# Sample attention stream: one cast per chunk on VectorE, and ScalarE's key copies and accumulator moves ahead of the exponential

## What is computed

```python
def fox_attention(q, k, v, fq, fk, q_pos, k_pos):      # one block of it
    s = jnp.einsum('bqhd,bkhd->bhqk', qi, k) * scale
    s = s + fi.transpose(0, 2, 1)[..., :, None] - fk_t[..., None, :]   # cumulative log forget values
    s = jnp.where(mask, s, -jnp.inf)
    p = jax.nn.softmax(s, axis=-1)
    return jnp.einsum('bhqk,bkhd->bqhd', p.astype(v.dtype), v)
```

## Time and profile before

| what | value |
|---|---|
| time, median of 3 runs | 4010.86 us (4007.85 to 4014.97) |
| the profiled execution | 4007.52 us |
| its span, first to last instruction | 4005.8 us |
| busy: TensorE, VectorE, ScalarE, GpSimd | 3686.3, 2013.1, 1706.0, 1070.8 us |
| granted TensorE clock, mean | 0.970 |
| GpSimd's `low_values` | 256 subtractions, 609.6 us |
| VectorE's `high_values` | 256 casts, 380.2 us |

### The profile page before, as it was taken

How to read it: one execution, slowest core, us unless ns; L and a number is a source line. 1 busy time by engine, 2 the same in 40 slices (tenths; PEclk the granted TensorE clock), 3 DMA queues, 4 the chain that set the end, 5 groups by cost and what they waited for, 6 DMA issues and landing times. The chain is left out here.

```text
span 4005.8 us, 55888 instructions
## 1 busy us (share of the span) xinstructions
PE 3686.3 (92%) x19019; PEld 2961.9 (74%) x19019; DVE 2013.1 (50%) x3175; ACT 1706.0 (43%) x3409; POOL 1070.8 (27%) x764
## 2 busy tenths in 40 slices
PE   8999999999999999988999996878888888699999
PEld 7788888887788888866787884555566666488887
DVE  3234433322134433214443436889898888744432
ACT  4224434554225335434344444555566666412222
POOL 0011222220011223201000003555566666422200
PEclk9999999999999999997998997989999999899999
DMA  4233343333233343313100007878898888644422
GB/s 157 99 108 116 121 148 131 118 116 105 94 124 131 127 158 106 128 57 95 43 1 12 12 1 257 259 240 265 256 297 286 279 284 285 228 159 165 166 84 82
DMA packets 354282, 590.76 MB, mean 147 GB/s; under 512 B 44029, under 2 KB 90213, under 8 KB 354026
## 3 DMA queue, kind: packets, MB, share of 16 engines
q1 hardware_dynamic: 340722, 576.00, 43.6%
q10 hardware_dynamic: 12736, 9.32, 0.8%
q0 software_dynamic: 576, 2.10, 0.1%
HBM read 475.38 MB, written 111.96 MB: 147 GB/s over the span
## 5 line engine op out<-in xcount | busy, mean ns | idle before, releaser
L853 PE MATMUL prj_z_ps<-prj_w_hi,prj_h_hi 128*128 128x512 f32 x2312 | 923.4, 399 | 2.6 <-DVE prj_w_lo L677 2.6
L855 PE MATMUL prj_z_ps<-prj_w_hi,prj_h_lo 128*128 128x512 f32 x2312 | 902.0, 390 | 0.0
L854 PE MATMUL prj_z_ps<-prj_w_lo,prj_h_hi 128*128 128x512 f32 x2312 | 900.8, 390 | 0.0
L1688 POOL TENSOR_TENSOR sa_v_lo<-sa_v_raw,sa_v_hi 128x1024 fp32r<-128x1024 f32 x256 | 609.6, 2381 | 416.7 <-DVE sa_v_hi L1860 416.7
L855 PEld LDWEIGHTS prj_z_ps<-prj_w_hi,prj_h_lo 128*128 128x128 f32 x2312 | 434.1, 188 | 93.6
L853 PEld LDWEIGHTS prj_z_ps<-prj_w_hi,prj_h_hi 128*128 128x128 f32 x2312 | 434.9, 188 | 89.7 <-DVE prj_w_lo L677 5.5
L854 PEld LDWEIGHTS prj_z_ps<-prj_w_lo,prj_h_hi 128*128 128x128 f32 x2312 | 435.0, 188 | 84.7
L2031 PE MATMUL sa_t_ps<-sa_ident,sa_k_raw 128*128 128x128 f32 x2048 | 315.0, 283 | 134.3 <-DVE sa_kT_lo L1852 134.3
L2031 PEld LDWEIGHTS sa_t_ps<-sa_ident,sa_k_raw 128*128 128x128 f32 x2048 | 246.6, 144 | 243.9 <-DVE sa_kT_lo L1852 126.7
L1852 DVE TENSOR_TENSOR sa_kT_lo<-sa_t_ps,sa_kT_hi 128x512 fp32r<-128x512 f32 x512 | 344.5, 682 | 109.7 <-ACT sa_kT_hi L1718 108.2
L1860 DVE CAST sa_v_hi<-sa_v_raw 128x1024 fp32r<-128x1024 f32 x256 | 380.2, 1485 | 2.0
(11 more groups left out here) (310 smaller groups left out, 5889.3 us busy)
## 6 DMA issues: line engine op xcount, KB each, us to landing
sa_k_raw<-in_cache_k_dram SPq DMA_DIRECT2D x512, 256.0 KB, 3.6
sa_v_raw<-in_cache_v_dram SPq DMA_DIRECT2D x512, 256.0 KB, 3.6
prj_w_raw<-in_w_main_dram SPq DMA_DIRECT2D x272, 256.0 KB, 4.1
z_scratch<-prj_z_sb SPq DMA_DIRECT2D x272, 256.0 KB
mo_mg<-z_scratch SPq DMA_DIRECT2D x51, 512.0 KB, 3.8
prj_cu<-extp_scratch SPq DMA_DIRECT2D x48, 256.0 KB
pa_raw<-z_scratch SPq DMA_DIRECT2D x12, 1024.0 KB, 10.7
prj_x_in<-in_x_all_dram SPq DMA_DIRECT2D x17, 512.0 KB, 3.7
```

The lines of the kernel that those rows point to most:

```text
L853: pe.matmul(out, h_hi[:, slot_of(t), k], hi, start=(k == 0), stop=False)
L854: pe.matmul(out, h_hi[:, slot_of(t), k], lo, start=False, stop=False)
L855: mm = pe.matmul(out, h_lo[:, slot_of(t), k], hi, start=False, stop=(k == KC - 1))
L1688: pool.tensor_tensor(v_lo[:, w % 2, at], v_raw[:, w % RING, at], v_hi[:, w % 2, at].bitcast(F32), ALU.subtract).then_inc(vlo_ready, 1)
```

## The change

VectorE casts the 128 x 2048 values of a chunk in one operation, which raises `vhi_ready` once, and GpSimd waits for it once and then subtracts both halves. On VectorE the cast stands where its second half stood, `low_keys(g, 1)` comes ahead of it, `running` (odd steps) and both `low` (even steps) stand between the two. On ScalarE `place` comes ahead of `move`; `exp` moves from behind `high(g, 1)` to behind `high(g, 2)`; `halves` and `halves_new` move from the end of the odd step to the start of the next even one. On TensorE the second half of `weigh` comes ahead of `turn_weights`. SyncE's program is the same.

```diff
@@ -1682,8 +1682,8 @@
                     pool.wait_ge(q_placed, 4 * n + 2 * (hh + 1))
 
             def low_values(w):
+                pool.wait_ge(vhi_ready, w + 1)
                 for half in range(2):
-                    pool.wait_ge(vhi_ready, 2 * w + half + 1)
                     at = slice(half * (CP // 2), (half + 1) * (CP // 2))
                     pool.tensor_tensor(v_lo[:, w % 2, at], v_raw[:, w % RING, at], v_hi[:, w % 2, at].bitcast(F32),
                                        ALU.subtract).then_inc(vlo_ready, 1)
@@ -1775,7 +1775,7 @@
             for g in range(G + 7):
                 n, c = divmod(g, CHUNKS)
                 odd = g % 2 == 1
-                s = (g - 3) // 2
+                s = (g - 3) // 2 if odd else (g - 4) // 2
                 if g == 1:
                     store_d(0)
                     act.wait_ge(new_step, 3)
@@ -1784,14 +1784,17 @@
                     act.wait_ge(d_stored, 32)
                     load_d(0)
                     load_d(1)
+                if not odd and is_seg(s):
+                    halves(s, 0)
+                    halves(s, 1)
+                    if first_seg(s):
+                        halves_new(s // PER)
                 if is_chunk(g):
                     high(g, 0)
                     high(g, 1)
-                if odd and is_seg(s):
-                    exp(s)
                 if is_chunk(g - 1):
+                    place(g - 1)
                     move(g - 1)
-                    place(g - 1)
                 if c == 1 and n < DEC_BATCH:
                     if n == 0:
                         act.wait_ge(cleared, CLEARED)
@@ -1801,15 +1804,13 @@
                     act.copy(addend_n[R:P], x_ps[R:P, 0:SAMPLE]).then_inc(new_moved, 1)
                 if is_chunk(g):
                     high(g, 2)
+                if odd and is_seg(s):
+                    exp(s)
+                if is_chunk(g):
                     high(g, 3)
                 if is_chunk(g - 1):
                     fetch(g - 1)
                     take(g - 1)
-                if odd and is_seg(s):
-                    halves(s, 0)
-                    halves(s, 1)
-                    if first_seg(s):
-                        halves_new(s // PER)
                 group, at = group_of(g)
                 if at == 8:
                     store_d(group)
@@ -1852,12 +1853,10 @@
                 dve.tensor_tensor(kT_lo[:, g % 2, :, at], heads_of(t_ps[:, j % 2]), kT_hi[:, g % 2, :, at].bitcast(F32),
                                   ALU.subtract).then_inc(klo_ready, 1)
 
-            def high_values(w, half):
-                if half == 0:
-                    dve.wait_ge(v_loaded[w % RING], 16 * CP * (w // RING + 1))
-                    wait_from(dve, weighed, w - 1)
-                at = slice(half * (CP // 2), (half + 1) * (CP // 2))
-                dve.tensor_copy(v_hi[:, w % 2, at], v_raw[:, w % RING, at]).then_inc(vhi_ready, 1)
+            def high_values(w):
+                dve.wait_ge(v_loaded[w % RING], 16 * CP * (w // RING + 1))
+                wait_from(dve, weighed, w - 1)
+                dve.tensor_copy(v_hi[:, w % 2], v_raw[:, w % RING]).then_inc(vhi_ready, 1)
 
             def take_new(n):
                 dve.wait_ge(new_added, n + 1)
@@ -1974,20 +1973,17 @@
                     low_keys(g, 0)
                 if odd and is_seg(s):
                     swap(s)
+                if is_chunk(g):
+                    low_keys(g, 1)
+                if odd and is_seg(s):
+                    running(s)
                 if not odd and is_seg(s):
                     low(s, 0)
-                if is_chunk(g - 3):
-                    high_values(g - 3, 0)
-                if odd and is_seg(s):
-                    running(s)
-                if is_chunk(g):
-                    low_keys(g, 1)
-                if not odd and is_seg(s):
                     low(s, 1)
                     if first_seg(s):
                         low_new(s // PER)
                 if is_chunk(g - 3):
-                    high_values(g - 3, 1)
+                    high_values(g - 3)
                 if g == 1:
                     dve.wait_ge(tok_loaded, 48)
                     dve.tensor_copy(vn_hi[:], tok[:, 2]).then_inc(pre_vector, 1)
@@ -2133,10 +2129,10 @@
                     turn(g, 3)
                 if is_chunk(g - 1):
                     third_pass(g - 1)
+                if is_chunk(g - 4):
+                    weigh(g - 4, 1)
                 if g % 2 == 1 and is_seg(s):
                     turn_weights(s)
-                if is_chunk(g - 4):
-                    weigh(g - 4, 1)
                 if c == 1 and n < DEC_BATCH:
                     lift_new(n)
                 group, at = group_of(g)
```

## The result

The changed kernel takes 3915.18 us (median of 4 runs, 3907.86 to 3917.63) against 4009.36 for the kernel before (median of 4, 4003.82 to 4014.97): a ratio of 0.9762, 95% interval 0.9743 to 0.9781, or 94 us less. The profiled span fell from 4005.8 to 3912.8.

What follows compares the result with a forecast made beforehand. VectorE was taken as the full engine, busy 12.99 of 14.27 us a pair of chunks. Savings of 51 (plain intervals), 4 (group intervals), 9 (last pairs) and 1 (start) make 65 us: 3946 us, range 3900 to 3990.

Steps and rivals of the forecast that it cites:

- the edits in order: ScalarE's reordering and TensorE's weigh ahead of turn_weights: no cost of their own; without cover, up to 1.0 us a pair.
- One cast: VectorE's single cast of a chunk takes 1.25 us, bounds 1.2 and 1.31, if it keeps the half's rate.
- The loop of cast and subtractions: VectorE's cast, then GpSimd's two subtractions: 6.1 us a chunk, 12.4 a pair with running, setting the beat.
- The change of sample: Every sixteenth chunk: stays at 5.7 us, plus one hold of 2.3 for the divide's second operation.
- The decay group: Extra work in the first three intervals: 29.5 us, with 3.5 a scan pair, giving 136.7 an interval, 1.5 less.
- The loads: K and V pages land at 17.6 us, wanted at 18.6: hidden, slack nearly used up, cost 0.
- the plain interval: Sixteen chunks and a change of sample without decay group: 107.2 us, 12.7 less; four give 51.
- Rival C: Every two-input VectorE operation waits for both GpSimd halves: 3 us less, 4008; chance 0.08.
- Rival A: Sample stream bound by transfers, floor near 13.3 us a pair: 30 us less, 3981; chance 0.20.
- rival B: Stalls vanish, TensorE sets 12.2 us a pair, the long subtraction holds nobody: 125 less, 3886; chance 0.08.
- D: K pages come late, with landings of 8 us: 24 us more, 4035; chance 0.05.
- E: The wide cast loses its rate, 2.4 us, 14.7 a pair: 4047; chance 0.04.

Runs made afterwards that it cites:

- e1: Kernel before with only the single 128x2048 cast and GpSimd waiting for it once, all other orders as before: 3970.47 us, ratio 0.9926.
- e2: Kernel before with only ScalarE's and TensorE's orders of the changed kernel, VectorE and GpSimd as before: 3981.01 us, ratio 0.9940.
- e8: Changed kernel with exp put back behind high 1, ahead of place and move: 3959.58 us, ratio 0.9883.
- e3: Changed kernel with the cast in two halves, one right behind the other, GpSimd waiting for each: 3915.93 us, ratio 0.9780.
- e4: Changed kernel with GpSimd's second subtraction 128x512 instead of 128x1024 from the third chunk on (output differs): 3882.83 us, ratio 0.9691.
- e12: e4 without the matmul of the fourth page's low values in each chunk from the third on (output differs): 3871.46 us, ratio 0.9655.
- e5: Changed kernel without the V page loads after the first three chunks (output differs): 3903.05 us, ratio 0.9745.
- e7: Changed kernel with the decay group's scans, whole and wide steps moved on VectorE to right behind the cast: 3890.87 us, ratio 0.9722.

## Why the prediction was right, and where its sizes were off

What bounds the kernel before: VectorE, by the cast held behind GpSimd. Half right. e1 and e2 show two bounds one right behind the other: the held cast, and ScalarE's chain from `running` over exp to the addend. The prediction counted both (2.03 us of TensorE's waits a pair), but set the edits in order to "cost nothing of their own" and never said what they bring; behind the cast all the orders together, VectorE's own included, are worth 94 - 34 = 60 us, and the place of exp alone 44 (e8).

One cast: 1.25 forecast, 1.21 measured. Right, and e3 shows why: no start of GpSimd falls in between.

The loop of cast and subtractions at 12.4 a pair: too large, and not the bound. Its shortest round is 6.0 us, since the next cast starts as soon as GpSimd lets go, and `running`'s hold (0.52 at the median) overlaps GpSimd's last stretch; 0.4 us of the 12.4 weren't there. TensorE sets the beat, 12.13 against the 12.2 to 12.3 laid out by hand; e4 and, for most of what was taken off, e12 show it. That two different bounds lie so close together is luck for the forecast. 0.27 us a pair over eight pairs is 2.2 us an interval.

The change of sample: 8.0 forecast, 104.1 - 8 x 12.13 = 7.0 measured. The one hold of the divide is there (2.35 us, 0.80 before, 0.49 free), on its first operation, but it isn't 2.3 us more of an interval: in the intervals at full clock the change of sample costs 102.8 - 97.0 = 5.8, as before, and the rest of the 7.0 is the clock's fall in the other two. e4 gives back 1.8.

The decay group: 29.5 forecast, 133.2 - 104.1 = 29.1 measured, and the scan pair 3.50 as assumed. The sum had no term for the clock, which is 0.89 to 0.92 in these intervals and was 0.91 to 0.95 before, so that 29.1 comes this close is luck in part.

The loads: hidden, with little slack. Right (7.2 us of waits in 450, and e5).

So the term that was mis-sized is the plain interval, 107.2 against 104.1, which also stands in the group's: 3.1 x 7 = 22 us of the 28 missing in the span; the merge stage's 4 and the start's 1 are most of the rest. Rival C's mechanism, a wait for both halves, was at work in part, at a price within the 3.5 us assumed: pairs took up to 4.75 us. The Trainium skill (SBUF — State Buffer, Who interferes with whom) says that whoever issues first gets the shared pair for the whole instruction. By the prediction's estimate from that rule every scan pair would have taken 2.3 us; three of the twelve come near it (2.35, 2.35 and 2.43), the others don't.

Rival A's floor of 13.3 us doesn't follow from its row: a share of 0.95 of 14.27 us is 13.6. Either is refuted by the pair of 12.13 at 335 GB/s, and by e5. Of rival B one half came true: TensorE sets the beat, 12.2 there, while the holds that it left out stayed; so the time came out between the forecast and B. Rivals D and E didn't happen: landings had a median of 3.9 us, and the cast kept its rate.

## What to carry to other kernels

Where VectorE and GpSimd share work on one tile, look for a VectorE operation that starts just after it has released GpSimd: give GpSimd its signal after the last of them, or put an operation with two SBUF inputs right behind, and read in the profile whether it begins ahead of the signalling one's end. Those that did (0.08 to 0.09 us ahead) ran free here; those that began 0.03 to 0.04 us after it ran free in three cases of seven. Before freeing a full engine, find the second bound and move both in one change: the cast brought 34 us alone and the orders of ScalarE and TensorE 23, the whole, with VectorE's order besides, 94. And read the granted clock of each interval before a few microseconds of it are put down to an edit.

## What was not expected of the hardware

- A start 0.04 us earlier in the profile doesn't decide: the divide's first operation began at 2719.47, GpSimd's at 2719.51, and the divide was held 2.70 us; at 2592.76 it began 0.05 us ahead of GpSimd and was free. The scans of e7, 0.16 us ahead of GpSimd or more, were not held (the first of each pair).
- The same wait of TensorE, 1.85 to 1.87 us, was followed by 3.4 us at a granted clock of 0.50 in two of four samples and by none in the other two.
- When GpSimd has two subtractions in a row and VectorE waits, the second scan of a pair is held to the end of the second one, so a queued GpSimd operation isn't kept off by VectorE's queue.
- Loads of K and V pages ran at 354 to 362 GB/s over 40 us at a DMA share of 1.02 to 1.04, where the kernel before moved 302 at 0.95. The share rose by a tenth while the rate rose by a fifth, so it says little of how much more can be moved.
